# Who makes the low parts of the masked decays in a chunked scan: ScalarE head by head, or GpSimd for eight heads at once

## The reference, cut to what matters

```python
a_cs = jnp.cumsum(dt * A, axis=2)
xdt = x * dt[..., None]
seg = a_cs[:, :, :, None] - a_cs[:, :, None, :]
decay = jnp.exp(jnp.where(lower, seg, -jnp.inf))
cb = jnp.einsum("bclgn,bcsgn->bclsg", Cm, Bm)
y_diag = jnp.einsum("bclsgj,bcsgjp->bclgjp", cb[..., None] * decay, xdt)
...
y_off = jnp.einsum("bclgn,bcgjpn->bclgjp", Cm, prev) * jnp.exp(a_cs)[..., None]
return (y_diag + y_off).reshape(b, s, g, j, p)
```

## Time and profile before

| | us |
|---|---|
| median of 3 runs | 3619.6 (3612.26 to 3623.09) |
| the profiled execution, its own time | 3616.24 |
| its span | 3614.4 |
| backward pass of the scan, in the span | to about 676 |
| forward pass, chunk 0 | 676 to 714 |
| forward pass, chunks 1 to 7, to the last `inside` | 714 to 892 |
| TensorE, VectorE, ScalarE, GpSimd busy over the span | 87%, 57%, 33%, 12% |

### The profile page before, as it was taken

The page is one execution under the profiler, slowest core; times in us unless marked ns, Lnnn a source line. Parts: engine busy times, 40 slices in busy tenths (PEclk is TensorE's granted clock), DMA queues, the critical chain, the costliest instruction groups (busy, mean ns, idle before and its releaser), DMA issues. The chain is left out here.

```text
span 3614.4 us, 37560 instructions
## 1 busy us (share of the span) xinstructions
PE 3141.3 (87%) x14208; PEld 2393.5 (66%) x14208; DVE 2060.6 (57%) x3113; ACT 1197.4 (33%) x2280; POOL 436.6 (12%) x407
## 2 busy tenths in 40 slices
PE   6999889886788879899997762989976989999999
PEld 5787667664677768677885552444554468888887
DVE  5112544487688835839886876549865334444444
ACT  2211231586566632234225651000264011112111
POOL 2000002344011100222340031010000000000000
PEclk9999999997899999999998986999988999999999
DMA  6323125433633334341462410411011011111111
GB/s 215 134 72 101 42 83 189 140 119 103 165 94 94 88 143 149 99 101 53 129 201 85 129 59 31 161 69 56 14 35 62 0 47 47 47 47 47 47 58 59
DMA packets 189934, 326.63 MB, mean 90 GB/s; under 512 B 16242, under 2 KB 110610, under 8 KB 189754
## 3 DMA queue, kind: packets, MB, share of 16 engines
q1 hardware_dynamic: 168602, 250.29, 22.7%
q0 software_dynamic: 21152, 73.94, 5.7%
HBM read 233.71 MB, written 89.16 MB: 89 GB/s over the span
## 5 line engine op out<-in xcount | busy, mean ns | idle before, releaser
L215 PE MATMUL banks<-b3h4a_hi,b3mlpw_part 128*128 128x512 f32 x1024 | 319.8, 391 | 6.8 <-DVE b3mlpw_part L3277 6.8
L215 PE MATMUL banks<-b3mlpw_part,b3mlp_acthi 128*128 128x512 f32 x1024 | 315.2, 389 | 0.0
L215 PE MATMUL banks<-b1ln_w,b_hThi 128*128 128x512 f32 x768 | 239.5, 393 | 0.0
L215 PEld LDWEIGHTS banks<-b3h4a_hi,b3mlpw_part 128*128 128x128 f32 x1024 | 193.7, 189 | 47.5 <-issue 7.1
L215 PEld LDWEIGHTS banks<-b3mlpw_part,b3mlp_acthi 128*128 128x128 f32 x1024 | 192.2, 188 | 39.9
L3324 DVE TENSOR_TENSOR b3out_x<-b3out_x,banks 128x1024 f32<-128x1024 f32 x128 | 154.8, 1219 | 111.6 <-PE banks L215 111.6
L215 PE MATMUL banks<-b3out_lo,b3mlpw_part 128*128 128x512 f32 x512 | 200.4, 391 | 0.0
L215 PE MATMUL banks<-b3mlpw_part,b3mlp_actlo 128*128 128x512 f32 x512 | 199.2, 389 | 0.0
L508 PE MATMUL banks<-b_hThi,b1item_hi 128*128 128x512 f32 x464 | 196.2, 423 | 3.4 <-DVE b1item_lo L497 3.1
L3294 ACT ACTIVATE b3mlp_relu<-banks 128x1024 f32<-128x1024 f32 x32 | 32.9, 1029 | 499.5 <-PE banks L215 499.5
L508 PE MATMUL banks<-b_hThi,b1item_lo 128*128 128x512 f32 x464 | 183.4, 395 | 0.0
(11 more groups left out here) (417 smaller groups left out, 6716.8 us busy)
## 6 DMA issues: line engine op xcount, KB each, us to landing
qk_spill<-b1scan_qk SPq DMA_DIRECT2D x64, 256.0 KB, 2.8
b1att_k<-qk_spill SPq DMA_DIRECT2D x64, 256.0 KB, 8.2
b1out_ws<-in_w_out SPq DMA_DIRECT2D x16, 1024.0 KB, 5.0
b3mlpw_stage<-in_w_mlp_up SPq DMA_DIRECT2D x16, 1024.0 KB, 5.3
b3mlpw_stage<-in_w_mlp_down SPq DMA_DIRECT2D x16, 1024.0 KB, 4.9
b2h_stage<-in_w_in SPq DMA_DIRECT2D x30, 512.0 KB, 4.1
b1item_stage<-in_w_in SPq DMA_DIRECT2D x29, 512.0 KB, 4.9
b1ln_stage<-in_w_in SPq DMA_DIRECT2D x12, 1024.0 KB, 6.8
```

The source lines that it names most:

```text
L215: last = pe.matmul(out, x, y, start=i == 0, stop=i == n - 1)
```

## The change

ScalarE makes only the high parts, buffers 0 and 2, 16 instructions for a unit. GpSimd makes the low parts, buffers 1 and 3, in a new helper `lows(c, gr)`: two instructions for a unit, each of 128x1024, mask (broadcast over eight heads) times `K.dtA_lo` (broadcast over 128 columns). Each `lows` but the first waits until the `tri` of the unit before has read the buffers. `tri` waits for the new semaphore `sc_low` besides `sc_L`. On GpSimd `lows(c,1)` stands ahead of `scaled`, the power and `weights(c,1)`, and `lows(c+1,0)` stands between `weights(c,1)` and `weights(c+1,0)`.

```diff
--- before.py
+++ after.py
@@ -914,6 +914,7 @@
             pe.wait_ge(S["sc_exp"], n)
         for half in range(2):
             pe.wait_ge(S["sc_L"], 2 * n + half + 1)
+            pe.wait_ge(S["sc_low"], 2 * n + 2)
             hs = slice(4 * half, 4 * half + 4)
             for i, (mask, part) in enumerate(((K.below, 0), (K.below, 1), (K.above, 2), (K.above, 3))):
                 last = pe.matmul(K.pair[1][:, half * 512:(half + 1) * 512], mask, m.R[part][:, hs], start=i == 0, stop=i == 3)
@@ -981,10 +982,10 @@
 
     def decays(c, gr, half):
 
-        for part, (table, mask) in enumerate(((K.dtA_hi, K.upper), (K.dtA_lo, K.upper), (K.dtA_hi, K.lower), (K.dtA_lo, K.lower))):
+        for d, mask in enumerate((K.upper, K.lower)):
             for j in range(4 * half, 4 * half + 4):
-                h = (part // 2) * 16 + gr * 8 + j
-                last = a.activation(m.R[part][:, j], mask, ACT.Copy, scale=table.bitcast(F32)[:, c, h:h + 1])
+                h = d * 16 + gr * 8 + j
+                last = a.activation(m.R[2 * d][:, j], mask, ACT.Copy, scale=K.dtA_hi.bitcast(F32)[:, c, h:h + 1])
         last.then_inc(S["sc_L"], 1)
 
     def exps(c, gr):
@@ -1052,6 +1053,17 @@
             dt = K.dt[:, c, d * 16 + gr * 8:d * 16 + gr * 8 + 8]
             g.tensor_tensor(to, over(dt, 2, P), over(m.cb[gr][d], 1, 8), ALU.mult).then_inc(S["sc_C"], 1)
 
+    def lows(c, gr):
+
+        n = 2 * c + gr
+        if n:
+            g.wait_ge(S["sc_tri"], n)
+        else:
+            g.wait_ge(S["dtA_lo"], 1)
+        for d, mask in enumerate((K.upper, K.lower)):
+            dtA = K.dtA_lo.bitcast(F32)[:, c, d * 16 + gr * 8:d * 16 + gr * 8 + 8]
+            g.tensor_tensor(m.R[2 * d + 1], over(mask, 1, 8), over(dtA, 2, P), ALU.mult).then_inc(S["sc_low"], 1)
+
     for b in range(ST):
         ch = ST - 1 - b
         if b < ST - 1:
@@ -1066,8 +1078,11 @@
         else:
             g.wait_ge(S["sc_xfree"], 1)
         K.stores.start(g, ("yb", ch), K.yb_dram[ch], m.y[b % 2])
+    lows(0, 0)
     weights(0, 0)
     for c in range(ST + 1):
+        if c < ST:
+            lows(c, 1)
         if c < ST - 1:
             scaled(ST + c)
         if c:
@@ -1077,6 +1092,7 @@
         if c < ST:
             weights(c, 1)
         if c + 1 < ST:
+            lows(c + 1, 0)
             weights(c + 1, 0)
         if c:
             use = K.misc_order.index(("turn", c - 1))
```

## The result

The changed kernel takes **3662.2 us** (median of 4 runs, 3657.2 to 3663.1) against 3620.3 for the kernel before: ratio 1.0113, 95% interval 1.0097 to 1.0129. The profiled execution took 3657.2 with a span of 3655.4, 41.0 longer than before. The forecast was 3655, slower, with a range from 3628 to 3682.

A forecast was written before the change was run, and what follows sets the result against it. The prediction took VectorE's queue to bound the forward pass, and ScalarE's loop only chunk 0. Terms 22.8 + 13.8 - 7.6 = +29 and +7 for the clock made +36, forecast 3655 us, range 3628 to 3682.

The forecast's parts named there:

- the meetings: VectorE and GpSimd instructions with SBUF inputs take turns in chunks 1 to 7: 22.8 us plus 13.8 us longer.
- the clock: Matmuls behind CB in chunks 1 to 4 run at 1.2 GHz after longer TensorE gaps: +7 us, between 0 and 13.
- chunk 0: The loop decays, tri, exp is the limit there; halving ScalarE's decays brings L1154 to 706.4 from 714.03, gain 7.6 us.
- Turn by turn: Low parts of (c,1) and `scaled` alternate with L1161 and two L1164, which end at 776.2 instead of 772.9.
- third rival: GpSimd's queue becomes the limit, low parts costing 2.41 us and holding up L1076 and the weights: +55, 3675; chance 17%.
- first place: Low parts of (c,1) meet L1161, two L1164 and L1148: 3.3 us in chunks 1 to 6, 3.0 in chunk 7.
- second place: Low parts of (c+1,0) meet L1143 and L1227, which wait 0.7 and 1.6: together 2.3 us in chunks 1 to 6.
- The low part's own cost, 1.89: Each GpSimd low part instruction takes 1.89 us, as L1053 of the same input form; 2.41 kept for the range.
- The rule weighed: By the skill's issue order L1161 would run first, each first place costing about 0.4 less, the sum 2.4 us lower.
- The signs: Expected: chunk 0's L1154 near 706, chunks of 32 to 36 us, five VectorE instructions 1 to 2 us longer, clock under 0.88.
- signs of being wrong: Low parts beside L1164 without lengthening it, VectorE idling for something other than GpSimd, or backward scan or attention changing length.
- Part 3: TensorE's clock: 1.2 GHz behind CB in chunks 1 to 4, falling in three of four, +7 us.

The follow-up runs named there:

- y earlier: The kernel before, with VectorE's two instructions adding the carried state's share to y moved ahead of the normalising: 3614.9 us, ratio 0.9986.
- stood alone: The changed kernel with GpSimd's low parts only in the first unit of each chunk, ScalarE making those of the second: 3638.0 us, ratio 1.0055.
- Keeping the clock up: The changed kernel plus 18 unread TensorE matmuls ahead of the next chunk's C times B in chunks 0 to 4: 3648.4 us, ratio 1.0078.
- the kernel cut in four: The changed kernel with each GpSimd low part instruction cut into four of 128 by 256: 3654.7 us, ratio 1.0101.

## Why the prediction was right, and where it was off

The pass explains the result: +47.5 us in chunks 1 to 7 and -3.2 in chunk 0 (37.00 to 33.84), of which 3.8 don't reach the span because the stage started that much earlier in this profiled execution (its first mask at 673.27 against 677.03). That start is not shown to be the change's doing: the kernel with y earlier, which is the kernel before up to there, has it at 674.81, so single executions differ here by microseconds. In the forecast's terms: 36.6 for the meetings, 7 for the clock and -7.6 for chunk 0 make 36; measured were 37.6, 9.9 and -3.2, which make 44.3. The medians lie 42 apart, and the forecast of 3655 was 7 us low by two mis-sized terms, chunk 0 and the clock, that erred the same way.

**VectorE is what the chunk waits for, and a faster ScalarE gives nothing beyond chunk 0**. Right, and shown: without the low parts the periods of chunks 1 to 7 didn't move.

**The meetings, 5.6 us a chunk and 3.0 in chunk 7.** Right in size: 5.9 and 6.4 in chunks 5 and 6, which have no quarters, and 2.9 in chunk 7. The way there was only partly the forecast one, so that the size came so near is in part luck. Turn by turn, as worked out from the earlier trace rows, with the successors of L1161 and both L1164 held, came in chunk 1 alone; in chunk 2 the gating waited for all three instructions of GpSimd in a row, and so it did in chunk 3 (7.37):

```profile
742.37 7.08 DVE L1177 TENSOR_TENSOR b1scan_y<-b1scan_y,b1scan_zg 128x1024 f32<-128x1024 f32 x1
742.74 1.91 POOL L1065 TENSOR_TENSOR b1scan_R<-fixed_upper,b1dtA_lo 128x1024 fp32r<-128x1024 f32 x1
744.59 1.90 POOL L1065 TENSOR_TENSOR b1scan_R<-fixed_lower,b1dtA_lo 128x1024 fp32r<-128x1024 f32 x1
746.45 1.91 POOL L1042 TENSOR_TENSOR b1scan_scaled<-b1scan_xs,b1ssm_dt_end 128x1024 f32<-128x1024 f32 x1
```

GpSimd lost nothing by it (1.91, 1.90, 1.91), so the power was early, and the sum came out near the same. In chunk 5 L1182, which the prediction didn't name at all, and the power's place in GpSimd's queue, part of the third rival's mechanism, carried 1.3 and 1.9 us of the first place. The second place was 2.28 for 2.3 beside the first, but when it stood alone it cost 3.5 in chunk 5: its price hangs on which VectorE instruction the low parts happen to meet.

**The clock, +7.** Right in mechanism, too small, and the clock fell in all four chunks, not in three: the four chunks with quarters are 9.9 us beyond the 5.6 (3.2, 3.7, 2.0, 1.0), near the 9.6 that was worked out and then cut because the clock was to fall in three of four. Keeping the clock up gave 8.1 us of these back, and 2.7 in chunk 0.

**Chunk 0, -7.6: the term that was mis-sized;** it came out at -3.2. With the stage's 3.76 us added to the times of after, the first exp is at 683.35 (forecast 683.5) and the second at 692.45 (694.0), so ScalarE's and TensorE's part held. The state is copied 1.7 us late, since L1159 took 2.90 us beside a low part and then L809 and L1170 stood ahead of L1164. CB(1) then stood behind a gap of 3.77 us and ran at 1.2 GHz, as did the quarter after it (granted 0.50 from 696.9 to 702.5), for which VectorE waited 4.84 us; with the clock kept up, chunk 0 was 2.7 us shorter. The prediction had priced the clock for chunks 1 to 4 only. The end of chunk 0:

```profile
703.89 0.69 DVE L809 TENSOR_TENSOR b1scan_qk<-banks,b1scan_qk 128x512 fp32r<-128x512 f32 x1 [4.84 <-ACT b1scan_qk L792]
...
707.11 0.68 DVE L1170 TENSOR_TENSOR b1scan_y<-b1scan_y,banks 128x512 f32<-128x512 f32 x1
```

Run with low parts in chunk 0 only, the gain was 6.6, close to the forecast.

**The low part's own cost, 1.89.** Right where it ran undisturbed (1.91); the estimate of 2.2 worked out from the Trainium skill's page (GPSIMD Engine Reference, Elementwise — side-by-side cycle accounting) is not borne out.

**The rule weighed.** The Trainium skill (SBUF — State Buffer, Who interferes with whom) lets the order of issue decide who blocks. L1177 started 0.37 us ahead of its low part and waited for it and for two more, so being first did not help it here; the measurement decides, and the 2.4 us were rightly not taken off. It isn't so everywhere: L1180 at 880.90 started 0.15 us ahead of a low part that came after a wait, took its usual 0.69, and the low part took 2.29.

**The signs.** L1154 of chunk 0 came at 707.11 for a forecast of 706, but that is the earlier start: counted from the same first mask it is 710.87. Chunks 1 to 6 came at 32 to 37 us, the clock is 0.81, and no wait of VectorE for an exp is left from 706 to 928. Of the five instructions named only L1161's and L1227's successors became 1 to 2 us longer; the others grew by 0.2 to 0.3. Of the signs of being wrong, one stayed away: what follows the pass, attention included, kept its length (2722.4 us before, 2722.8 now). One came in two chunks: an L1180 of chunk 6 and one of chunk 7 ran beside a low part and kept their 0.69 us. And VectorE did idle for something other than GpSimd: it waited 16.8 us for L792, the copy of a quarter's result, instead of 10.0. That is the forecast clock term at work, so this sign contradicted the prediction's own Part 3.

## To carry to other kernels

Busy shares don't tell which engine to relieve; what an engine's result waits for after it is ready does. Work moved to GpSimd that reads SBUF is paid by VectorE's instructions with SBUF inputs, and smaller pieces only move the bill to GpSimd's queue; so in this kernel it pays where VectorE's queue is short (one chunk of eight, 6 us won) and in no other chunk. Not tried: the low parts behind the power in GpSimd's queue, which would spare the 1.9 us of waiting for it. Price a longer gap of TensorE together with the matmuls that follow it, in every stage where it grows.

## What the runs showed of the hardware beyond what was expected

- A VectorE instruction that meets a run of GpSimd instructions can wait for the whole run (7.08 us for three), or for one of them (2.46 for 0.69 in chunk 5). The thirteen traces here, from 560 to 935 us, tell the cases apart (VectorE instructions without PSUM input; a run is GpSimd tensor instructions without a gap). VectorE began at least 0.05 us ahead, and GpSimd began after a wait: none of 49 was held, and GpSimd paid (2.72 for 1.90 at 567.26). VectorE began ahead, and the run stood straight behind GpSimd's own start of a DMA, as the first place does with the store L128: 53 of 71 were held, all but one to the end of the whole run, and the 18 others were within 0.31 us of their end. VectorE began inside a run with more to come: all 65 that were held waited for the running instruction alone (memsets and the kernel cut in four not counted). Why the start of a DMA changes it, no run shows.
- The smallest instruction is held as well: 128x2 with one SBUF input took 1.74 us instead of 0.17, to 0.03 us after the low part's end. It was held beside memsets too (1.32), where instructions with two SBUF inputs were not; but there the product behind it began 0.08 us later and took its usual 1.24, so that this hold cost VectorE nothing.
- GpSimd's memsets hold no VectorE instruction with two inputs: 0.69 and 1.24 in the middle of them.
- GpSimd's power of 128x2 took 0.71 us straight behind another instruction and 1.64 after a wait.
- 18 unread matmuls in the gap ahead of CB raised TensorE's granted clock in chunks 1 to 4 from 0.80, 0.86, 0.90 and 0.90 to 0.89, 0.90, 0.90 and 0.95, and made the kernel 13 us faster, 9.7 to 9.9 of it in the pass.
